# One mixer block on one core: first head by input tiles, projections one head ahead, output product beside the last attention

## What is computed

```python
mod = c @ ada_w[l] + ada_b[l]
sh1, sc1, gt1, sh2, sc2, gt2 = [m[:, None, :] for m in jnp.split(mod, 6, axis=-1)]
h = rmsnorm(x, norm1_g[l]) * (1.0 + sc1) + sh1
p = h @ w_in[l]
xr, yr, q, k, v, ga, gb = jnp.split(p, cuts, axis=-1)
xr = causal_dwconv(xr, conv_w[l], conv_b[l])
y_a = rg_lru(xr, rg_wa[l], rg_ba[l], rg_wx[l], rg_bx[l], rg_lambda[l]) * jax.nn.gelu(yr)
q = head_rmsnorm(q.reshape(b_, s_, ATT_HEADS, HEAD_DIM), q_norm_g[l])
k = head_rmsnorm(k.reshape(b_, s_, ATT_HEADS, HEAD_DIM), k_norm_g[l])
v = v.reshape(b_, s_, ATT_HEADS, HEAD_DIM)
y_b = stick_breaking_attention(q, k, v)
mix = jax.nn.sigmoid(ga) * y_a + jax.nn.sigmoid(gb) * y_b
x = x + gt1 * (mix @ w_out[l])
```

## Time and profile before

| | |
|---|---|
| median of 3 runs | 2004.64 us (2003.0 to 2004.96) |
| the profiled execution | 2001.63 us |
| its span, first to last instruction | 1999.9 us |
| PE busy | 1927.0 us (96%) |
| DVE, ACT, POOL busy | 955.9, 855.5, 795.3 us (48, 43, 40%) |
| bytes moved | 202.62 MB, mean 101 GB/s |

### The profile page before, as it was taken

The page is one execution under the profiler, slowest core; times in us unless marked ns, Lnnn a source line. Parts: engine busy times, 40 slices in busy tenths (PEclk is TensorE's granted clock), DMA queues, the critical chain, the costliest instruction groups (busy, mean ns, idle before and its releaser), DMA issues.

```text
span 1999.9 us, 25272 instructions
## 1 busy us (share of the span) xinstructions
PE 1927.0 (96%) x8704; PEld 1564.6 (78%) x8704; DVE 955.9 (48%) x1108; ACT 855.5 (43%) x1156; POOL 795.3 (40%) x355
## 2 busy tenths in 40 slices
PE   2999999998999999999999999999999999999998
PEld 2777777776788888888888888787776788888886
DVE  5666666666644343222344331446776544344322
ACT  2566666664455554223222222356766333222221
POOL 4233333334344444443444444443332434444443
PEclk9999999999999999999999999999999999999999
DMA  7233333332222232222222323222222122222332
GB/s 277 99 122 121 122 125 126 126 127 81 78 94 94 97 102 94 95 94 95 95 94 95 98 101 105 86 83 84 73 73 74 64 94 95 94 94 94 106 105 74
DMA packets 54470, 202.62 MB, mean 101 GB/s; under 512 B 6048, under 2 KB 6176, under 8 KB 53536
## 3 DMA queue, kind: packets, MB, share of 16 engines
q1 hardware_dynamic: 54432, 202.10, 29.8%
HBM read 199.98 MB, written 2.10 MB: 101 GB/s over the span
## 4 chain that ended last, share of the span: by engine, by line
PE 92%; DVE 4%; ACT 1%; issue 1%; POOL 1%; DMA 1%; SPq 0%; DVEq 0%; POOLq 0%; ACTq 0%
PE bank L569 27%; PE bank L574 27%; PE bank L570 27%; PE bank L822 1%; PE bank L824 1%; PE bank L823 1%; PE bank L684 1%; PE bank L658 1%; DVE MIX L1304 1%; PE bank L693 1%; PE bank L855 1%; POOL SS L470 1%; DMA XT<-in_xt 1%; DVE HL L1304 0%; PE bank L893 0%
## 5 line engine op out<-in xcount | busy, mean ns | idle before, releaser
L478 POOL TENSOR_TENSOR WL<-ring,WH 128x1024 fp32r<-128x1024 f32 x309 | 756.4, 2448 | 1146.2 <-ACT WH L972 1146.0
L569 PE MATMUL bank<-HH,WL 128*128 128x512 f32 x1864 | 744.1, 399 | 8.7 <-ACT HH L988 3.8
L972 ACT ACTIVATE WH<-ring 128x1024 fp32r<-128x1024 f32 x317 | 335.8, 1061 | 934.0 <-PE bank L574 873.7
L570 PE MATMUL bank<-HH,WH 128*128 128x512 f32 x1864 | 731.5, 392 | 0.0
L574 PE MATMUL bank<-HL,WH 128*128 128x512 f32 x1864 | 463.6, 390 | 1.0 <-DVE HL L1304 1.0
L569 PEld LDWEIGHTS bank<-HH,WL 128*128 128x128 f32 x1864 | 353.4, 190 | 87.6 <-issue 9.6
L570 PEld LDWEIGHTS bank<-HH,WH 128*128 128x128 f32 x1864 | 353.6, 190 | 76.2 <-issue 3.8
L574 PEld LDWEIGHTS bank<-HL,WH 128*128 128x128 f32 x1864 | 350.7, 188 | 76.3 <-DVE HL L1304 3.6
L570 PE MATMUL bank<-FH,WH 128*128 128x512 f32 x544 | 211.6, 389 | 0.0
L569 PE MATMUL bank<-FH,WL 128*128 128x512 f32 x544 | 211.6, 389 | 0.0
L574 PE MATMUL bank<-FL,WH 128*128 128x512 f32 x544 | 135.0, 389 | 0.0
(11 more groups left out here) (277 smaller groups left out, 1841.0 us busy)
## 6 DMA issues: line engine op xcount, KB each, us to landing
ring<-in_stream SPq DMA_DIRECT2D x365, 512.0 KB, 3.3
ARENA<-in_ada SPq DMA_DIRECT2D x6, 1024.0 KB, 18.6
XT<-in_xt SPq DMA_DIRECT2D x1, 2048.0 KB, 12.7
result<-XT SPq DMA_DIRECT2D x3, 512.0 KB, 2.7
result<-XT SPq DMA_DIRECT2D x2, 256.0 KB, 2.0
vec<-in_vec SPq DMA_DIRECT2D x1, 220.0 KB, 2.6
```

Of the source, the lines that this page charges most:

```text
L478: nc.gpsimd.tensor_tensor(WL[:, slot, :], ring[:, u % RING, :], WH[:, slot, :].bitcast(F32), ALU.subtract).then_inc(w_low, 1)
L569: mm(out_ap, part(WL, base, loc, k), xh(k), start=(start and k == 0), stop=False)
L570: mm(out_ap, part(WH, base, loc, k), xh(k), start=False, stop=False)
L972: A(WH[:, split_at(base, loc)[1], :], ring[:, u % RING, :], ACT.Copy).then_inc(w_high, 1)
```

## The change

**Start.** The first modulation comes in 4 groups (`GROUPS`) of 4 column blocks, two for the shift and two for the scale, each enough for two input tiles. SP loads x first, then the groups (2 MB each) between the first weight units. The first head's weights are laid out by input tile: unit k holds the blocks of all 7 projections for tile k, 896 columns. PE runs 21 matmuls per tile into 7 banks that stay open. DVE does the additions that POOL did, the group sums (`first_rows`) and the low part of these weights (`first_low`); POOL waits until all 8 are done.

**Heads.** In the loop (now 7 rounds) the projections are those of the next head, set between the steps of this head's attention. The gate products are split into parts like the others: 6 matmuls on `XCH`, `XCL` in place of two plain fp32 ones.

**Last head.** In place of projections PE runs the output product, for 7 of 8 input tiles, into all banks as they come free. The eighth (the last head's own) follows in `out1_end`, for 6 output tiles in one piece.

```diff
+FIRST = ("ga", "q", "k", "gb", "v", "xr", "yr")
+FIRST_BANK = (0, 5, 7, 1, 2, 3, 4)
+FIRST_COLS = len(FIRST) * P
+Q, K, ADA0, ADA1, GATES, XR, ADA2, ADA3, V, YR, GA, GB = range(HEAD_UNITS)
+HEAD_SPLIT = {_loc: _n for _n, _loc in enumerate((Q, K, GATES, XR, V, YR, GA, GB))}
 HEAD_ADA = (ADA0, ADA1, ADA2, ADA3)
-HEAD_ORDER = (Q, K, V, XR, YR, GA, ADA0, ADA1, ADA2, ADA3, GATES, GB)
-HEAD_DONE = {_loc: _n + 1 for _n, _loc in enumerate(HEAD_ORDER)}
+O0, O1, O2, O3, O4, O5, K7, O6, O7 = 0, 1, 5, 8, 9, 10, 11, 12, 13
+LAST_SPLIT = {_loc: _n for _n, _loc in enumerate((O0, O1, GATES, O2, O3, O4, O5, K7, O6, O7))}
+OUT1_BANK = (0, 1, 6, 5, 7, 3, 4, 2)
...
+            for p in range(GROUP_BUFFERS):
+                first_group(p)
+                if 2 * p < RING:
+                    first_unit(2 * p)
+                    first_unit(2 * p + 1)
+            for k in range(RING, KD):
+                sp.wait_ge(w_low, k - RING + 1)
+                first_unit(k)
+                if k == RING + 1:
+                    sp.wait_ge(first_sum, KD - 1)
+                    first_group(GROUP_BUFFERS)
...
+            out1_split(O0)
+            pool.wait_ge(unit_done, DONE + SPLIT_BEFORE[U_LAST])
+            pool.wait_ge(q["mix_done"], HEADS - 1)
+            for k in range(4, KD - 1):
+                nc.gpsimd.tensor_copy(tile_of(HH, k), tile_of(MIX, k)).then_inc(out1_high, 1)
+            out1_split(O1)
+            out1_split(GATES, 2 * P)
...
+            first_columns(0)
+            pe.wait_ge(rs0_copied, 1)
+            for k in range(KD):
+                def first_part(W, j):
+                    return W[:, k % 2, j * P:(j + 1) * P]
+                pe.wait_ge(w_low, k + 1)
+                pe.wait_ge(h_high, k + 1)
+                if k < KD - 1:
+                    for j, b in enumerate(FIRST_BANK):
+                        if k % 2 and j == 4:
+                            first_columns((k + 1) // 2)
+                        mm(bank[b][:, :], first_part(WL, j), tile_of(HH, k), start=(k == 0), stop=False)
+                        mm(bank[b][:, :], first_part(WH, j), tile_of(HH, k), start=False, stop=False)
+                    pe.wait_ge(h_low, k + 1)
+                    for j, b in enumerate(FIRST_BANK):
+                        last = mm(bank[b][:, :], first_part(WH, j), tile_of(HL, k), start=False, stop=False)
+                    last.then_inc(unit_done, 1)
+                else:
+                    pe.wait_ge(h_low, k + 1)
+                    for j, b in enumerate(FIRST_BANK):
+                        mm(bank[b][:, :], first_part(WL, j), tile_of(HH, k), start=False, stop=False)
+                        mm(bank[b][:, :], first_part(WH, j), tile_of(HH, k), start=False, stop=False)
+                        last = mm(bank[b][:, :], first_part(WH, j), tile_of(HL, k), start=False, stop=True)
+                        last.then_inc(first_done if j < len(FIRST) - 1 else unit_done, 1)
...
+            def gates(h, base, i, stride):
+                split_wait(base, GATES, i, per_iteration(base, stride))
+                pe.wait_ge(q["xch_done"], h + 1)
+                pe.wait_ge(q["rq_done"], h + 1)
                 pe.wait_ge(q["rk_done"], h + 1)
...
+                for b in (5, 7):
+                    mm(bank[b][:, :], part(WL, base, GATES, b // 7), M["XCH"], start=True, stop=False)
+                    mm(bank[b][:, :], part(WH, base, GATES, b // 7), M["XCH"], start=False, stop=False)
+                pe.wait_ge(q["xcl_done"], h + 1)
+                for b in (5, 7):
+                    last = mm(bank[b][:, :], part(WH, base, GATES, b // 7), M["XCL"], start=False, stop=True)
+                last.then_inc(unit_done, 1)
...
+                pe.wait_ge(q["sga_done"], h + 1)
+                proj(0, Q)
                 pe.wait_ge(q["sgb_done"], h + 1)
...
+                proj(1, K)
+                scores(h)
+                gates(h, U_HEAD, h, HEAD_UNITS)
+                pe.wait_ge(q["q_evac"], 2 * h + 4)
+                proj(0, XR)
+                pe.wait_ge(q["k_evac"], 2 * h + 4)
+                proj(1, V)
+                suffix(h)
+                pe.wait_ge(q["rg_sig"], h + 1)
+                proj(5, YR)
+                pe.wait_ge(q["ig_sig"], h + 1)
+                values(h, 7)
+                pe.wait_ge(q["xr_evac"], h + 2)
+                proj(0, GA)
+                pe.wait_ge(q["gy_done"], h + 2)
+                q_square(h + 1)
+                pe.wait_ge(q["yb_done"], h + 1)
+                k_square(h + 1)
+                v_rows(h + 1)
+                proj(1, GB)
+                head_ada(h)
...
+            h = HEADS - 1
+            pe.wait_ge(q["sga_done"], h + 1)
+            out1(0, ready=True).then_inc(unit_done, 1)
+            pe.wait_ge(q["sgb_done"], h + 1)
+            out1(1).then_inc(unit_done, 1)
+            scores(h)
+            gates(h, U_LAST, 0, 0)
+            head_ada(h)
+            pe.wait_ge(mod_done, GROUPS + 1)
+            out1(2).then_inc(unit_done, 1)
+            pe.wait_ge(q["rg_sig"], h + 1)
+            out1(3).then_inc(unit_done, 1)
+            suffix(h)
+            pe.wait_ge(q["ig_sig"], h + 1)
+            out1(4).then_inc(unit_done, 1)
+            values(h, 2)
+            out1(5).then_inc(unit_done, 1)
+            split_wait(U_LAST, K7)
+            pe.wait_ge(out1_high, 4)
+            pe.wait_ge(h_low, LOW[8] + KD)
+            for m in range(5):
+                out1_end(m).then_inc(out1_done, 1)
+            out1_end(5).then_inc(unit_done, 1)
+            out1(6)
+            out1_end(6).then_inc(unit_done, 1)
+            pe.wait_ge(q["yb_done"], h + 1)
+            out1(7)
+            out1_end(7).then_inc(unit_done, 1)
...
+                finished(Q)
+                act.wait_ge(q["qn_done"], h + 1)
+                A(M["QR"], bank[0][:, :], ACT.Copy).then_inc(q["q_evac"], 1)
+                A(M["QSQ"], bank[0][:, :], ACT.Square).then_inc(q["q_evac"], 1)
+                high_of(GATES)
+                finished(K)
+                high_of(XR)
+                act.wait_ge(q["kn_done"], h + 1)
+                A(M["KR"], bank[1][:, :], ACT.Copy).then_inc(q["k_evac"], 1)
+                A(M["KSQ"], bank[1][:, :], ACT.Square).then_inc(q["k_evac"], 1)
+                absolute(h)
+                finished(GATES)
+                high_of(V)
+                log_part(h)
+                gate_parts(h)
+                finished(XR)
+                high_of(YR)
+                act.wait_ge(q["conv_done"], 4 * h + 4)
+                A(M["XR"][:, 3:3 + S], bank[0][:, :], ACT.Copy).then_inc(q["xr_evac"], 1)
+                p_high(h)
+                finished(V)
+                high_of(GA)
+                A(M["VF"], bank[1][:, :], ACT.Copy).then_inc(q["v_evac"], 1)
+                multiplier(h)
+                weights_of_v(h)
+                conv_high(h + 1)
+                finished(YR)
+                high_of(GB)
+                act.wait_ge(q["ya_done"], 2 * h + 1)
+                A(M["GY"], bank[5][:, :], ACT.Gelu_apprx_tanh).then_inc(q["gy_done"], 1)
+                finished(GA)
+                high_of(HEAD_UNITS + Q)
+                act.wait_ge(q["ya_done"], 2 * h + 2)
+                A(M["SGA"], bank[0][:, :], ACT.Sigmoid).then_inc(q["sga_done"], 1)
+                q_root(h + 1)
+                k_root(h + 1)
+                v_turned(h + 1)
+                finished(GB)
+                act.wait_ge(q["yb_done"], h + 1)
+                A(M["SGB"], bank[1][:, :], ACT.Sigmoid).then_inc(q["sgb_done"], 1)
+                high_of(HEAD_UNITS + K)
...
+            def first_low(k):
+                dve.wait_ge(w_high, k + 1)
+                TT(WL[:, k % 2, 0:FIRST_COLS], ring[:, k % RING, 0:FIRST_COLS], WH[:, k % 2, 0:FIRST_COLS].bitcast(F32),
+                   ALU.subtract).then_inc(w_low, 1)
+            for k in range(1, KD):
+                dve.wait_ge(sq0_done, k + 1)
+                if k > 1:
+                    dve.wait_ge(sum0_done, k - 1)
+                TT(SS[:, :], tile_of(MIX, 0) if k == 1 else SS[:, :], tile_of(MIX, k), ALU.add).then_inc(sum0_done, 1)
+            first_rows(0, 1, 4)
+            first_rows(0, 4, KD)
+            first_low(0)
+            for p in range(GROUPS):
+                dve.wait_ge(ada_col, 4 * (p + 1))
...
+                TT(shift_and_scale(MOD[:, 0:2 * KD]), shift_and_scale(bank[6][:, 0:2 * KD]), shift_and_scale(v("ada_b", 0, 2 * KD)),
+                   ALU.add).then_inc(mod_done, 1)
+                dve.wait_ge(mod_done, p + 1)
+                at = slice(2 * p, 2 * p + 2)
+                STT(G1[:, at], MOD[:, KD + 2 * p:KD + 2 * p + 2], one[:, :], v("norm1_g", 2 * p, 2), ALU.add, ALU.mult).then_inc(gain_done, 1)
+                dve.wait_ge(gain_done, p + 1)
+                dve.wait_ge(rs0_copied, 1)
+                for k in (2 * p, 2 * p + 1):
+                    STT(tile_of(MIX, k), tile_of(XT, k), G1[:, k:k + 1], SQ[:, :], ALU.mult, ALU.mult).then_inc(h_mul, 1)
```

(30 more changed lines are left out.)

586 lines of the change are left out of this document (344 added, 242 removed).

## The result

The changed kernel takes 2011.62 us, the median of six runs (2008.80 to 2018.78); the kernel before, run beside it, 2004.11 us (2001.75 to 2004.96). The ratio is 1.0042, with a 95% interval of 1.0028 to 1.0055: slower, by 7.5 us or 0.4%. The profiled execution took 2011.57 us, of which the span is 2009.5; before, 2001.6 and 1999.9.

What follows compares the result with a forecast made beforehand. PE, 96% busy, was taken as the bound. Start, first head and loop sum to 444.8 us; 75 for the last stage and 1.5 for half clock give 521.3, 4.2 later than before: 2008.8 us, range 1994 to 2021.

Steps and rivals of the forecast that it cites:

- the likeliest case: Whole kernel: the forecast itself, 2008.8 us, slower by 4.2, own range 2005 to 2013; chance 0.34.
- First product: Start of the kernel: PE's first product at 27.0 us, 25.3 us earlier than before.
- First head: From first product to v's squares and transpose: waits of some 2.9 us, two clock falls at 1.9, over at 84.0.
- Loop: Seven rounds between first and last head: 51.3 us each, 359.1 in all, including waits for low parts and values.
- First round: First of the seven rounds: DVE late by two reciprocals and SP late in loading V, 1.7 us.
- Last head: Last head and output product: PE's own work 53.1 us plus waits, PE through at 63.5 us into the stage.
- Residual: End of the output product: DVE's instructions wait for POOL's splits, 7 to 9 us more; last tile squared at 75.
- The mark: Moment when the last token sums ahead of the feed-forward part begin: 521.3 us against 517.1.
- the one by which DVE and POOL hardly meet: Faster: POOL's splits hardly delay DVE; 13 us earlier, 15 with one clock fall; 1994 to 1996; chance 0.30.
- The clock staying up: No change: waits as forecast, but no clock falls at the groups and the mark; -5.3 us, 2003.5; chance 0.18.
- The rival to which I gave only 0.06: Slower: three clock falls, not two, in the first head and one in the first output product; +3.8, 2012.6; chance 0.06.
- V's unit: Slower: SP holds V's load in every round, 1.5 us a round and a later split; +10 us, 2019; chance 0.08.

Runs made afterwards that it cites:

- one combined kernel: Changed kernel with all repairs, modulation's units in their old place in the last head, DVE's low parts ahead of k's norm: 1990.27 us, ratio 0.9939.
- the next: The same repairs and low parts ahead of k's norm, plus filler products of 10, 6, 5 and 8 where PE still waits: 1984.24 us, ratio 0.9910.
- the last: The filled kernel with DVE's low parts of the seven mixed tiles behind k's norm again: 1984.16 us, ratio 0.9898.
- the first: Changed kernel with repairs of residual, first head, suffix and V together, and ACT's root ahead of a weight copy: 1987.81 us, ratio 0.9920.

## Why the prediction was right, and where it was not

The forecast was 2008.8 and slower by a little; the measured 2011.6 lies inside the range and inside the likeliest case's own range of 2005 to 2013. That it lies so near is in part luck, since errors of 4 us in both directions cancel. Step by step:

- **First product:** 27.0 forecast, 25.57 measured. Right, and 1.4 too long, as the seven additions were done at 15.7 and not at 17.2.
- **First head:** waits of 2.9 forecast, 2.73 to 2.86 measured, and for the reason given. Mis-sized: I counted two falls of the clock and there were three, and the last cost 3.1 us, not 1.9 (66.81 to 83.17 against 13.3), so that the head's products ended at 83.2, not at 81.8, though they had begun 1.4 earlier. DVE's work in a round, 11.2, was right; its waiting was 4.1 us (1.3 and 2.9), not 2.1, since it waits for a PE at half clock, and with the fall each round is 15.2, as the sum of 13.3 and 1.9 had it.
- **Loop:** 51.3 forecast, 51.21 measured. The 0.3 for the values wasn't there. The wait of 0.5 for PL was, and it was worth more than itself: without it the round is 50.4.
- **First round:** V late by 1.7 forecast, 3.39 measured, and the clock fell behind it (seven products of 0.43 us from 110.5 to 113.5), 1.4 more, which the prediction had at nothing.
- **Last head:** PE through at 63.5 us into this stage forecast, 62.1 measured (449.0 to 511.1). Two sums of mine don't hold: 53.1 of work and 9.9 of waits are 63.0, and 53.1 fits eight output tiles at 4.77, not the seven that I wrote, beside the 10.0 that the small parts took. Its waits were mis-sized: the first output product ended 9.7 into the stage, not 11.7, and all waits in the stage were 7.2 for my 9.9.
- **Residual:** it ends 8.6 behind PE, where I had 11.5. My own terms, 49, 16.4 and 7 to 9, give 72.4 to 74.4 and not the 75 that I wrote. Measured from the first update, it took 22.9: the 16.4, and 6.5 for POOL's splits, a little under my 7 to 9.
- **The mark:** 521.3 forecast, 521.7 measured. The stage began 4.2 late (449.0 for 444.8), its last square was done 4.3 sooner into it than forecast, and the token sums behind it took 0.5 longer. That they cancel to 0.4 is luck.
- **What failed** is the sentence that everything behind 517.16 is the same program, so that the forecast is of this one moment. The same program took 1.6 us longer up to the feed-forward part's first product, since PE came to it at 1.2 GHz, and in this profile 3.4 us longer after it, of which one fall of the clock behind 24 narrow products was 3.2. Medians differ by 7.5 us, the marks by 4.5, the spans of the two profiled executions by 9.6.

Of the rivals, the one by which DVE and POOL hardly meet is out: they met in every round (PL took 2.13 us in place of 1.49) and in the residual. The clock staying up is out as well. The rival to which I gave only 0.06, three falls in the first head and one in the first output product, is what happened, and its 2012.6 is nearer to 2011.6 than my 2008.8; the fall in the output product cost little, since PE had DVE's low parts to wait for there (they ended at 458.29, the product at 458.68). V's unit was late in the first round alone. The expected gain of 25 us at the start did arrive (26.8) and was spent in the first head, the loop and the residual. None of the three losses was in the nature of the change: an order in DVE's queue, one copy in ACT's and eight squares on the wrong engine held them. With these, V's unit and ACT's root moved the same plan is 0.8% faster than the kernel before, and with fillers 0.9 to 1.0%. What stays open is why PE waited 1.0 us for the values in three rounds of one combined kernel, in two of the next, in one of the last and in none of the first, and what decides behind which of the short waits the clock falls and how long it stays down.

## What to carry to other kernels

When work is moved ahead of its inputs, lay out the queue of the engine that feeds it instruction by instruction: an instruction that waits in the middle of it (here a weight split behind ACT behind PE) idles all that follow, and its idle time is then the bound. Count a DVE instruction that reads two tiles in SBUF and a POOL one that does the same as one after the other, and put sources in PSUM or work on ACT beside POOL instead. Price a stretch at half clock behind each wait of PE, fill such a wait if its cause can't be moved, and compare stages, not totals, where a few microseconds decide.

## What was not expected of the hardware

- One program, two clocks: with the same instructions the first head took 57.6 us from first product to squares in one kernel and 62.1 in another (25.57 to 83.17, 25.54 to 87.60). In these seven kernels a round between two groups took 15.1 to 16.8 us with its fall, against 13.6 with the wait filled.
- The clock also fell with PE never idle, behind 24 products of one column. It did so in 5 of the 14 profiles (granted clock 0.64 to 0.82 in the 8 us behind them, 1.00 in the other nine), and at the same place of the second block in 9 of 14, the kernel before among them. From the products to the spread behind them it took 8.2 us without a fall, and 9.8 or 11.4 with one.
- Idle time made the difference at the groups, not the narrow products there: useless products in place of the waits kept the clock up nine times out of nine, in three kernels. In the two that have a partner without them they paid for themselves (5.1 us at the end of the first head, 3.3 at the first feed-forward product).
- DVE's reciprocal is untouched by POOL: 3.34 us from 449.94, with POOL's split running from 450.46 to 452.85.
